# Output projection, second half: twelve of sixteen half tiles as 2x2 block products made of seven block products

## What is computed

```python
P  = xn @ w_in[l]
A  = attention(...) * SiLU(gate_A)        # 1024 columns
B  = Bg * conv3(Cg * h) * SiLU(gate_B)    #  512 columns
C  = gla(...) * SiLU(gate_C)              #  512 columns
x  = x + gate * concat(A, B, C) @ w_out[l]
```

## Time and profile before

| | |
|---|---|
| median of 3 runs | 2119.91 us (2119.39 to 2120.05) |
| span of the profiled execution | 2118.3 us |
| TensorE busy in it | 98% |
| VectorE busy | 70% |
| ScalarE busy | 31% |
| GpSimd busy | 8% |
| TensorE in the chain that ended last | 95% |
| mean granted TensorE clock | 0.999 |

### The profile page before, as it was taken

How to read it: one execution, slowest core, us unless ns; L and a number is a source line. 1 busy time by engine, 2 the same in 40 slices (tenths; PEclk the granted TensorE clock), 3 DMA queues, 4 the chain that set the end, 5 groups by cost and what they waited for, 6 DMA issues and landing times.

```text
span 2118.3 us, 33687 instructions
## 1 busy us (share of the span) xinstructions
PE 2084.8 (98%) x13031; PEld 1854.6 (88%) x13031; DVE 1487.4 (70%) x2921; ACT 646.9 (31%) x1100; POOL 173.2 (8%) x118
## 2 busy tenths in 40 slices
PE   5999999999999999999999999999999999999998
PEld 4788888888999999999998888888899999999998
DVE  5879789999666667866475455566666666677776
ACT  4232221311333334442043222232133333354312
POOL 0000000000000000523310000000000000043321
PEclk9999999999999999999999999999999999999999
DMA  9989687664333324664445647444343233266444
GB/s 365 388 303 341 211 282 261 233 222 161 115 106 104 106 71 130 201 208 142 128 129 166 189 127 216 144 143 146 109 128 107 74 101 107 86 213 214 149 120 154
DMA packets 357334, 365.43 MB, mean 173 GB/s; under 512 B 17670, under 2 KB 264156, under 8 KB 356572
## 3 DMA queue, kind: packets, MB, share of 16 engines
q1 hardware_dynamic: 328528, 320.67, 47.2%
q10 hardware_dynamic: 28684, 43.09, 5.4%
HBM read 304.98 MB, written 58.72 MB: 172 GB/s over the span
## 4 chain that ended last, share of the span: by engine, by line
PE 95%; DVE 2%; DMA 1%; issue 1%; ACT 0%; ACTq 0%; SPq 0%; DVEq 0%
PE psP L926 30%; PE psP L999 8%; PE psT L938 8%; PE psO L1008 7%; PE psP L996 6%; PE psP L994 6%; PE psP L995 6%; PE psP L1001 4%; PE psT L1008 4%; PE psP L1193 3%; PE psO L1239 3%; PE psT L1204 2%; PE psO L968 1%; DMA wmod<-in_w_mod_dram 1%; DVE r_a L2124 1%; PE psP L1056 1%
## 5 line engine op out<-in xcount | busy, mean ns | idle before, releaser
L926 PE MATMUL psP<-x_pair,high 128*128 128x512 f32 x1704 | 546.7, 391 | 0.0
L926 PEld LDWEIGHTS psP<-x_pair,high 128*128 128x128 f32 x1704 | 319.8, 188 | 70.5 <-issue 3.4
L926 PE MATMUL psP<-x_pair,low 128*128 128x512 f32 x852 | 331.8, 389 | 0.0
L1485 ACT ACTIVATE high<-raw 128x1024 fp32r<-128x1024 f32 x128 | 135.4, 1059 | 590.8 <-PE psT L938 504.2
L2025 DVE SCALAR_TENSOR_TENSOR macc<-mraw,cond,macc 128x128 f32<-128x128 f32 (+1 forms) x810 | 308.7, 455 | 0.0
L2043 DVE TENSOR_TENSOR low<-raw,high 128x1024 fp32r<-128x1024 f32 x128 | 157.1, 1228 | 172.9 <-ACT high L1485 172.8
L999 PE MATMUL psP<-x_pair,high 128*128 128x512 f32 x512 | 200.9, 392 | 0.0
L926 PEld LDWEIGHTS psP<-x_pair,low 128*128 128x128 f32 x852 | 160.0, 188 | 33.0 <-issue 0.5
L994 PE MATMUL psP<-x_pair,high 128*128 128x384 f32 x512 | 180.2, 352 | 0.0
L996 PE MATMUL psP<-x_pair,low 128*128 128x384 f32 x512 | 172.2, 336 | 0.0
L995 PE MATMUL psP<-x_pair,high 128*128 128x384 f32 x512 | 171.7, 335 | 0.0
(11 more groups left out here) (359 smaller groups left out, 4040.1 us busy)
## 6 DMA issues: line engine op xcount, KB each, us to landing
raw<-in_w_in_dram SPq DMA_DIRECT2D x132, 512.0 KB, 5.1
wmod<-in_w_mod_dram SPq DMA_DIRECT2D x32, 1024.0 KB, 8.6
mraw<-in_w_mod_dram SPq DMA_DIRECT2D x64, 512.0 KB, 4.2
mraw<-in_w_mod_dram SPq DMA_DIRECT2D x32, 1024.0 KB, 7.4
raw<-in_w_in_dram SPq DMA_DIRECT2D x32, 1024.0 KB, 5.5
raw<-in_w_out_dram SPq DMA_DIRECT2D x64, 512.0 KB, 4.0
old<-x_scratch SPq DMA_DIRECT2D x64, 320.0 KB, 2.9
xf<-proj_scratch SPq DMA_DIRECT2D x48, 320.0 KB, 3.3
```

The lines of the kernel that those rows point to most:

```text
L926: mm = pe.matmul(latent_ps[m], own, moved, start=(k == 0 and w is whole and x is x_high), stop=(k == KT - 1 and x is x_low))
L1485: act.activation(ring(high, l, n), ring(raw, l, n), ACT.Copy).then_inc(s["chunk_cast"], 1)
```

## The change

Twelve of the sixteen half tiles (tiles 2 to 13, six pairs) are no longer computed one by one. A pair of output tiles by 640 tokens is a 2x2 block matrix (two tiles by two halves of 320 tokens), and the sum over eight k is cut in even and odd k: weights 2x2 blocks `B`, tokens 2x2 blocks `A`. Such a product takes eight block products; the change computes it from seven, of sums and differences of the blocks (Winograd's form). Tiles 0, 1, 14 and 15 stay as they were.

- Weights: GpSimd forms four sums a pair (`quad_sums`: 512 elements each, in `raw` and `rstd`), ScalarE casts the seven blocks (`quad_cast`), VectorE makes their low parts (`quad_rest`), into eight places of `high` and `low`.
- Tokens: once in each layer GpSimd forms four sums (`token_sums`: three quarters of each, 960 elements, as soon as the first GLA pair is out and the convolution done; 320 elements after the last), ScalarE casts seven blocks of 1280 elements (`token_cast`), VectorE makes the low parts (`token_rest`).
- Products: `seventh(q)` for q = 0 to 41, twelve matmuls of 320 columns each, into one of eight PSUM half banks; before q it waits for the low part of its weights (`block_split`) and, from q = 8, for the join that frees the bank.
- Joins: thirteen VectorE operations a pair add the seven products up and onto the residual, which is now loaded straight into `xf` (`kept_in`), and ScalarE copies one product (`corner_copy`).
- `split_half` is left for tiles 1, 14 and 15; `old_x` for tiles 0, 1, 14, 15. Each 512 KB load of `w_out` is as before. `add_square` keeps its place on GpSimd, behind the sums of the next pair.
- Semaphores are renamed and shared in other stages, to make room for the new ones; their waits have the same meaning.

```diff
+QUAD = HALF_K // 2
+SEVEN = 7
+B11, B21, T2, T1, B22, T3, T4 = range(SEVEN)
+A11, A12, S2, S1, S4, S3, A22 = range(SEVEN)
+SEVEN_PAIRS = range(1, OUT_PAIRS - 1)
...
+PRODUCTS = SEVEN * len(SEVEN_PAIRS)
+JOINS = 13
+JOIN_OF = (0, 1, 2, 7, 4, 6, 10)
...
+WEIGHT_PLACES = (6, 7, 2, 3, 0, 1, 4, 5)
...
+        product_banks = [bank[:, at:at + HALF] for bank in (psO, psP[0], psP[1], psT) for at in (0, 512)]
...
+    def quad_weights(i):
+        at = i % 2 * HALF_K
+        for j in range(2):
+            if i < 3:
+                sp.wait_ge(s[f"split{j}"], occ + SECOND + i - 1 + SEED)
+            else:
+                sp.wait_ge(s["block_split"], weights_split(l, SEVEN * (i - 2)))
+            sp.dma_start(raw[j][:, at:at + HALF_K, :], w_out[:, HALF_K:, (2 * i + j) * P:(2 * i + j + 1) * P])\
+                .then_inc(s[f"quad_in{i % 2}"], 16)
+    def kept_in(i):
+        if l > 0 or i > 1:
+            sp.wait_ge(s["kept_in"], 16 * (l * len(SEVEN_PAIRS) + i - 1))
+        sp.wait_ge(s["block_split"], tokens_split(l, {1: S1 + 1, 2: S4 + 1, 3: S3 + 1}.get(i, SEVEN)))
+        sp.dma_start(xf[:, 2 * i:2 * i + 2, :], x_dram[:, 2 * i:2 * i + 2, :]).then_inc(s["kept_in"], 16)
...
+    quad_weights(1)
     for j in range(2):
         sp.wait_ge(s[f"x_part{j}"], 16 * (l + 1) * OUT_PAIRS + SEED)
         old_x(j, 0)
-    with sp.Fori(1, OUT_PAIRS - 1) as i:
-        second_weights(1, i)
-        sp.wait_ge(s["taken0"], i + occ + SECOND + SEED)
-        old_x(0, i)
-        second_weights(0, i + 1)
-        sp.wait_ge(s["taken1"], i + occ + SECOND + SEED)
-        old_x(1, i)
-    second_weights(1, OUT_PAIRS - 1)
+    quad_weights(2)
+    kept_in(1)
+    kept_in(2)
+    kept_in(3)
+    quad_weights(3)
+    sp.wait_ge(s["mix_split"], (l + 1) * KT)
+    kept_in(4)
+    kept_in(5)
+    kept_in(6)
     for j in range(2):
-        sp.wait_ge(s[f"taken{j}"], OUT_PAIRS - 1 + occ + SECOND + SEED)
+        sp.wait_ge(s[f"taken{j}"], occ + SECOND + 1 + SEED)
         old_x(j, OUT_PAIRS - 1)
+    quad_weights(4)
+    quad_weights(5)
+    quad_weights(6)
+    for j in range(2):
+        second_weights(j, OUT_PAIRS - 1)
...
+    def seventh(q):
+        idx, out = q % SEVEN, product_banks[q % len(product_banks)]
+        pe.wait_ge(s["block_split"], weights_split(l, q + 1))
+        if q >= len(product_banks):
+            wait_joined(q - len(product_banks))
+        elif 2 <= q < 6:
+            pe.wait_ge(s[f"taken{q // 2 - 1}"], occ + SECOND + 1 + SEED)
+        whole, rest = weight_place(high, q), weight_place(low, q)
+        for k in range(QUAD):
+            for w, x in ((whole, token_high), (whole, token_low), (rest, token_high)):
+                mm = pe.matmul(out, w[:, k, :], x[idx][:, k, :], start=(k == 0 and w is whole and x is token_high),
+                               stop=(k == QUAD - 1 and w is rest))
+        mm.then_inc(s["product_done"], 1)
+    for q in range(PRODUCTS):
+        seventh(q)
+    n = occ + SECOND + 1
+    for q in range(PRODUCTS - 8, PRODUCTS - 6):
+        wait_joined(q)
+    half_tile(2, psP[0], n, ("taken0", n + SEED))
+    for q in range(PRODUCTS - 6, PRODUCTS - 4):
+        wait_joined(q)
+    last_half_tile(3, psP[1], n)
...
+    def token_cast(idx):
+        if idx == A11:
+            act.wait_ge(s["tile_done1"], occ + SECOND + SEED)
+        if idx in (S1, S2, S4, S3):
+            act.wait_ge(s["block_summed"], tokens_summed(l, {S1: 5, S2: 6, S4: 7, S3: 8}[idx]))
+        act.activation(token_high[idx][:], token_source(idx), ACT.Copy).then_inc(s["block_cast"], 1)
+    def quad_cast(q):
+        i, idx = SEVEN_PAIRS[q // SEVEN], q % SEVEN
+        if idx == B11:
+            act.wait_ge(s[f"quad_in{i % 2}"], 32 * (l * (len(SEVEN_PAIRS) // 2) + (i + 1) // 2 if i % 2 else
+                                                    l * (len(SEVEN_PAIRS) // 2) + i // 2))
+        if idx in (T1, T3, T2, T4):
+            act.wait_ge(s["block_summed"], weights_summed(l, q // SEVEN, {T1: 1, T3: 2, T2: 3, T4: 4}[idx]))
+        if q >= len(WEIGHT_PLACES):
+            act.wait_ge(s["product_done"], l * PRODUCTS + q - len(WEIGHT_PLACES) + 1)
+        else:
+            act.wait_ge(s[("tile_done1", "tile_done0", "tile_done0", "tile_done1")[q // 2]],
+                        occ + SECOND + q // 4 + SEED)
+        act.activation(weight_place(high, q), weight_source(i, idx), ACT.Copy).then_inc(s["block_cast"], 1)
...
+    def corner_copy(m):
+        act.wait_ge(s["product_done"], l * PRODUCTS + SEVEN * m + 1)
+        if m > 0:
+            act.wait_ge(s["joined"], JOINS * (l * len(SEVEN_PAIRS) + m - 1) + 3)
+        act.activation(corner, product_banks[SEVEN * m % len(product_banks)], ACT.Copy)\
+            .then_inc(s["corner_copied"], 1)
...
+    for idx in range(SEVEN):
+        token_cast(idx)
+        quad_cast(idx)
+    for m in range(len(SEVEN_PAIRS)):
+        for idx in range(SEVEN):
+            if m + 1 < len(SEVEN_PAIRS):
+                quad_cast(SEVEN * (m + 1) + idx)
+            if idx == 0:
+                corner_copy(m)
+            if idx in (2, 3):
+                square(m, idx - 2)
+    for slot in range(2):
+        square(len(SEVEN_PAIRS), slot)
...
+    def token_rest(idx):
+        dve.wait_ge(s["block_cast"], tokens_split(l, idx + 1))
+        dve.tensor_tensor(token_low[idx][:], token_source(idx), token_high[idx][:].bitcast(F32), ALU.subtract)\
+            .then_inc(s["block_split"], 1)
+    def quad_rest(q):
+        dve.wait_ge(s["block_cast"], weights_split(l, q + 1))
+        dve.tensor_tensor(weight_place(low, q), weight_source(SEVEN_PAIRS[q // SEVEN], q % SEVEN),
+                          weight_place(high, q).bitcast(F32), ALU.subtract).then_inc(s["block_split"], 1)
...
+    def join(m, idx):
+        i, base = SEVEN_PAIRS[m], JOINS * (l * len(SEVEN_PAIRS) + m)
+        first, second = 2 * i, 2 * i + 1
+        def product(n):
+            return product_banks[(SEVEN * m + n) % len(product_banks)]
+        def gate(tile, v):
+            return mod[:, tile + 2 * KT, v:v + 1]
+        def early(tile, src):
+            dve.scalar_tensor_tensor(xf[:, tile, 0:HALF], src, gate(tile, 0), xf[:, tile, 0:HALF], ALU.mult, ALU.add)\
+                .then_inc(s["joined"], 1)
+        def late(tile, src):
+            for v, part in ((0, slice(HALF, DEC)), (1, slice(DEC, TOK))):
+                dve.scalar_tensor_tensor(xf[:, tile, part], src[:, part.start - HALF:part.stop - HALF], gate(tile, v),
+                                         xf[:, tile, part], ALU.mult, ALU.add).then_inc(s["joined"], 1)
+        dve.wait_ge(s["product_done"], l * PRODUCTS + SEVEN * m + idx + 1)
+        if idx == B11:
+            dve.wait_ge(s["kept_in"], 16 * (l * len(SEVEN_PAIRS) + m + 1))
+            dve.wait_ge(s["corner_copied"], l * len(SEVEN_PAIRS) + m + 1)
+            early(first, product(B11))
+        elif idx == B21:
+            dve.wait_ge(s["joined"], base + 1)
+            early(first, product(B21))
+        elif idx == T2:
+            dve.tensor_tensor(both, product(T2), corner, ALU.add).then_inc(s["joined"], 1)
+        elif idx == T1:
+            dve.wait_ge(s["joined"], base + 3)
+            dve.tensor_tensor(upper, product(T1), both, ALU.add).then_inc(s["joined"], 1)
+        elif idx == B22:
+            dve.wait_ge(s["joined"], base + 4)
+            dve.tensor_tensor(upper, product(B22), upper, ALU.add).then_inc(s["joined"], 1)
+            dve.wait_ge(s["joined"], base + 5)
+            early(second, upper)
+        elif idx == T3:
+            dve.tensor_tensor(both, product(T3), both, ALU.add).then_inc(s["joined"], 1)
+            dve.wait_ge(s["joined"], base + 7)
+            dve.tensor_tensor(lower, product(T1), both, ALU.add).then_inc(s["joined"], 1)
+            dve.wait_ge(s["joined"], base + 8)
+            late(second, lower)
+        else:
+            dve.tensor_tensor(upper, both, product(T4), ALU.subtract).then_inc(s["joined"], 1)
+            dve.wait_ge(s["joined"], base + 11)
+            late(first, upper)
+    split_half(1, occ + SECOND, whole + OUT_PAIRS)
+    for idx in range(SEVEN):
+        token_rest(idx)
+        quad_rest(idx)
+        if idx in (S2, S1):
+            finish(idx - S2)
+    for m in range(len(SEVEN_PAIRS)):
+        for idx in range(SEVEN):
+            if m + 1 < len(SEVEN_PAIRS):
+                quad_rest(SEVEN * (m + 1) + idx)
+            elif idx == T3:
+                split_half(2, occ + SECOND + 1, whole + OUT_PAIRS + 1)
+            join(m, idx)
+            if l + 1 == DEPTH and idx in (B22, T3):
+                weigh(2 * m + idx - B22)
+    split_half(3, occ + SECOND + 1, whole + OUT_PAIRS + 1)
+    if l + 1 == DEPTH:
+        for slot in range(2):
+            weigh(2 * len(SEVEN_PAIRS) + slot)
+    finish(KT - 2)
+    finish_last()
...
+    def token_sums(first, last, base):
+        part = slice(first, last)
+        for n, (idx, one, other, op) in enumerate((
```

(35 more changed lines are left out.)

250 lines of the change are left out of this document (140 added, 110 removed).

## The result

The changed kernel takes 2165.5 us (median of 4 runs, 2162.6 to 2166.9), against 2119.65 us (2118.8 to 2120.1) for the kernel before on the same chip: a ratio of 1.0215, with a 95% interval of 1.0201 to 1.023.

A forecast was written before the change was run, and what follows sets the result against it. The prediction took VectorE, stopped by GpSimd on the shared SBUF port, as the new bound: losses of 24.7 and 29.8 us added to the 2118.3 us span, plus 1.6 us to the runs' median, gave 2174.4 us, range 2144 to 2195.

The forecast's parts named there:

- TensorE's price: TensorE's matmuls in the seven products: 1.77 us a product, 12.4 us a pair, saving 17.8 us over two layers.
- as it is meant: Rival: TensorE stays the bound in the rounds and the kernel gains 17.8 us, to 2102 us; chance 0.06.
- The exclusion, and VectorE as the bound: In the rounds, GpSimd instructions hold the shared SBUF port, stopping VectorE 4.9 us a round; VectorE becomes the bound.
- VectorE's own work: Seven quad_rest and thirteen join operations with their waits: 10.97 us a pair on VectorE, 11.9 in the last layer.
- The start: First layer's beginning: token sums hold up mix_low until 13.3 us, tile 1 ends at 23.4; 13.5 us lost by product 7.
- The end of the stretch: First layer's last tiles: 5.6 us lost ahead of tile 14, then tiles 14 and 15 take 13.9 us.
- worse, by the clock: Rival: an underfed TensorE gets a lower clock, adding 5 to 12 us a layer, 2184 to 2198 us; chance 0.07.
- The sum: Loss over both stretches: 24.7 us in the first layer, 29.8 in the last, together 54.5 us.
- Which operations are held: Only VectorE operations with two SBUF inputs were counted on the shared port; weigh was priced at 0.54 us.
- The releaser: Sign: products with TensorE idle ahead of them would be released by VectorE's low.
- half: Rival: token_sums comes too late to meet mix_low, only rounds are long: +17.1 and +22.2 us, 2159 us; chance 0.12.
- The handover rule: Rival: each shared-port handover costs some 115 ns after the blocking instruction ends; +71 us, 2191 us; chance 0.04.

The follow-up runs named there:

- experiment 2: The changed kernel with GpSimd's token sums, weight sums and additions of squares all replaced by writes of constants: 2100.6 us.
- experiment 1: The changed kernel with GpSimd's four weight sums per pair replaced by writes of a constant: 2122.7 us.
- experiment 7: The changed kernel with only GpSimd's additions of squares replaced by writes of a constant: 2142.9 us.
- experiment 9: The changed kernel with the four weight sums per pair moved from GpSimd to VectorE: 2159.7 us.
- experiment 10: The changed kernel with weight sums and additions of squares both moved from GpSimd to VectorE: 2153.4 us.
- experiment 3: The changed kernel with the join sums regrouped so that T1's PSUM bank is free after the fourth join operation, not the eighth: 2165.3 us.
- after: The changed kernel itself, as the study measured and profiled it: 2165.5 us.
- experiment 4: The changed kernel with GpSimd's token sums begun only when all sixteen mix_low are done: 2172.2 us.
- experiment 8: The changed kernel with GpSimd's four weight sums per pair replaced by copies of one of their two operands: 2134.1 us.
- experiment 5: The changed kernel with every join operation on VectorE cut to one column per part: 2139.5 us.

## Why the prediction was right, and where it was off

- **TensorE's price: right.** With nothing in the way (experiment 2) the 42 products take 74.2 us, 1.767 us each; 1.77 was said. That kernel's 2100.6 us is the rival "as it is meant", 2102.
- **The exclusion, and VectorE as the bound: right**, and shown by experiments 1, 2, 7, 9 and 10. The 84 `quad_rest` have a mean of 1.26 us; over 1.1 was the sign named. Their own time is 0.68 us, not 0.74. (A slip in a row: the operation of 1.92 us in the earlier trace rows takes 0.81 us when free, not 0.87; nothing was worked out from it.) The stops in the round of 1025 us are 0.85, 0.93, 0.99, 0.98 and 1.10 us at five rests, and 0.52 at the join with two SBUF operands: 5.4 us. 4.9 was said.
- **VectorE's own work: the term that was mis-sized.** I gave it 10.97 us. The round of 15.04 less 5.4 us of stops is 9.7 us; the 14.05 us of experiment 10 less its four sums and two squares (4.4 us from start to start) are 9.65. From start to start a rest takes 0.60 us (0.66 said), a join of two PSUM and SBUF operands 0.40 (1030.20 to 1030.60 in experiment 1; 0.46 said), and an operation that waits for the one before it 0.11 us more (0.24 said). The prices came from the earlier trace rows, whose operations have a third operand: on that form (L2751) 0.46 us is right. So the rounds are 15.04 us, not 15.8.
- **The start: right in its size.** From the end of the last matmul ahead (972.51), the last `mix_low` ends after 13.45 us (13.3 said), and the first product starts after 23.3 (23.4 said). Product 7 ends after 41.4 us, where the prediction's sum comes to 39.8. One cause is in the trace: the fifth product waits 2.16 us for `low` and then runs while the granted clock is 0.57 (1005 to 1009 us).
- **The end of the stretch.** Tile 14 starts after 116.9 us (121.9 by the prediction's 135.8 less 13.9), since the rounds were shorter. Tiles 14 and 15 take 15.8 us, not 13.9: after 3.35 us of waiting for `split_half` the granted clock falls.

```profile
1091.00:1095.00 4.00, 4.00 (x17) 3.77 (x17) 2.66 (x5) 2.33 (x3) 2.29 (x1) 0.62 0.74 247
```

- In experiment 1, where that wait is 0.92 us, they take 14.2 us. So the clock cost 1.6 us there. The rival "worse, by the clock" had 5 to 12 us a layer. Its mechanism occurs more often than it costs: in the first layer the granted clock is also 0.50 in most of tile 0 (976 to 981 us, after a wait of 4.32 us), which then waits for `mix_low` all the same, and 0.57 from 1022 to 1026 us, after the wait of 2.58 us in a round. In the rounds it costs nothing (experiment 3), so it is left with the fifth product and tiles 14 and 15, a fraction of the size.
- **The sum.** The first layer's stretch is 132.6 us against 111.0: +21.6, with +24.7 said. By the parts of the prediction: +15.1 up to product 7 (13.5 said), +10.2 in the 35 products after it (14.5), +3.4 ahead of tile 14 (5.6), +1.9 in tiles 14 and 15 (none), less 8.9. The stretch of the last layer, read in the same way (up to the last matmul of tile 15), is 141.5 us against 115.4: +26.1, with +29.8 said; its rounds take 15.9 us, with 16.8 said. The spans differ by 44.7 us: the first stretch begins 2.5 us sooner in after, in code that the change leaves alone, and among the runs of this study it begins anywhere from 972.5 to 976.3 us, so I take that for scatter; the rest is under 0.5 us. The total came nearer than its terms, in part by luck: in each round VectorE's own work was put 1.3 us too high and the stops 0.5 us too low, and tiles 14 and 15 were given nothing.
- **Which operations are held: too narrow.** The prediction gave `weigh` its 0.54 us and had only operations with two SBUF inputs held. In after it is held in four rounds, for 1.0 us each; the rest that would have met the same sum isn't, so the round hardly shows it.
- **The releaser: wrong.** Said was `low`. The list of waits names L2781, and after that is taken away (experiment 3) it names `low`, at the same time. Both hang on one queue.
- **The rival "half": wrongly worked out.** I priced late token sums at 2159 us by dropping the early stops and leaving the rest as it was. The sums still need 17 us on GpSimd; experiment 4 gave 2172.2.
- **The handover rule: not seen.** By that figure of the Trainium skill (SBUF — State Buffer, "A bandwidth-pool intuition that's wrong"), some 115 ns pass after the blocker's end; the page measured it for GpSimd's writing of descriptors behind a VectorE copy. Here a rest ends 0.55 us after the sum that held it, less than the 0.60 us from start to start of a free one. With GpSimd second, the square from 1028.11 ends 1.44 us after the rest of 1027.09 does, and a free square takes 1.54 us (1085.35). The measurement decides: nothing visible either way.

Open: the parts of the last layer's loss were not followed row by row. That experiment 1 came out 5 us under its layout is open too; TensorE is the bound there by a little, and it may be that small misses on VectorE no longer show, but no run tests this. And that a write of GpSimd stops `weigh` rests on one row.

## What to carry to other kernels

Before work is given to an idle GpSimd, list which of its operations read SBUF and which of VectorE's take two SBUF operands, and look in a trace for others that are held, as `weigh` is: where they meet, their times add up as on one engine, and a GpSimd sum costs twice what it costs on VectorE (1.27 against 0.60 us for 512 elements). If VectorE is near the bound, try the sum in VectorE's own queue; here it was cheaper there. If VectorE has slack, as in the kernel before, such an overlap needn't cost anything. And read a wait's releaser as a question: move the dependency, and see whether the time or only the name changes.

## What the runs showed of the hardware

- GpSimd's plain copy of 512 elements takes 0.61 us and a write of a constant 0.53 us, against 1.27 to 1.30 us for a sum of two operands. One operand read excludes VectorE's two-operand work as two do, for half as long; a write does not (experiments 8 and 1).
- VectorE's `tensor_scalar` from SBUF to SBUF, with one tile operand (`weigh`, 640 elements), is held too: 0.55 us alone, 1.55 to 1.59 beside a sum. Beside a write it took 0.88 us, in the one row where it came second (experiment 2).
- An operation of VectorE on a single column is held as well, if it has two SBUF operands: two of them lasted 1.21 us beside a sum, and 0.35 us without one (experiment 5).
- A VectorE operation from PSUM with one other operand (`tensor_tensor`, 320 columns) passes every 0.40 us, the one with a gate as third operand every 0.46 to 0.47 us.
